# A decoder trunk on Trainium2: U and V expert rows gathered together as 8 KB into five joint buffers, and dense tiles loaded in pairs

## The chip, the cores and the metric

One core of one Trainium2 chip runs the whole kernel. The metric is the device time of one execution, in microseconds. Everything is float32.

## What is computed

Two layers of a hybrid decoder on 512 tokens of width 1024. The mixers (attention, gated DeltaNet, S5) come first in a layer; the change does not touch them. After them comes the PEER layer, cut here to what matters:

```python
def block(xt):                       # 128 tokens
    qry = (xt @ w_query).reshape(128, 8, 2, 128)
    ...                              # 16 of 16384 experts for each of 8 heads: idx, gate
    act = jax.nn.gelu(jnp.einsum('td,thkd->thk', xt, expert_u[idx]))
    return jnp.einsum('thk,thkd->td', gate * act, expert_v[idx])
```

and then a gated embedding, `x = x + sigmoid(rms_norm(x, ple_norm) @ ple_w_gate) * (pe @ ple_w)`. `expert_u` and `expert_v` have 16384 rows of 1024 numbers (4 KB) each per layer.

## The kernel before

**Two ways through PEER.** Half of the 512 tokens (tiles 0 and 1) go the dense way, on TensorE: all 16384 experts are multiplied, in 128 tiles of 128 experts. The unit is the *pair* of such tiles: `pre(p)` multiplies the U tiles of pair p with the tokens (32 matmuls, L1721), ScalarE takes the gelu into one of 12 buffers `act_pair` (L1937), VectorE multiplies it by dense gates (L2133, L2136), and `values(p)` multiplies it with the V tiles (16 matmuls, L1733). SyncE loads the U tiles one by one into four buffers (aT, sT and the halves of bT, L1806) and the V tiles into four slots of `v_tile` (L1827); each load waits until the tile that had its buffer was used. A tile is 512 KB, a row of it 4 KB for each of 128 partitions.

The other half (tiles 2 and 3) goes the sparse way, with rows fetched from the tables. A *row* n is one of 16 choices of one head for 128 tokens: 128 table rows of 4 KB, 512 KB, for U and as much for V. There are 256 rows n in a layer. GpSimd fetches them with indirect DMAs (`fetch`, L2198) into five buffers `u_rows` and five buffers `v_rows`. VectorE makes the *dot* of a U row with the normed tokens (L2093; its line shows as CUSTOM_DVE_ANT_0, or ISA in an order) and later the *addition* of the V row times its weight onto x (L2105).

**Chunks.** Four rows are a *chunk*, 64 in a layer. In chunk c VectorE makes the four dots of c, ScalarE one gelu of four columns (L1909), and VectorE the weights (L2099) and the four additions of chunk c - LAG, with LAG = 2. A U buffer is free after its dot, a V buffer after its addition.

**The order** is one list, made by `tail_order`, which each engine follows in its own code. Steps that matter here:

- First the *hot* steps, 32 of them: VectorE builds one-hot tiles (L2120, L2122), TensorE multiplies them (L1708), ScalarE copies the sums (L1922) and stores them in four stores of 2 MB, `dense_gates` (L1925), in pieces of 1 KB. Chunks 0 to 3 stand behind every eighth hot step, so chunk 3 stands just ahead of the last copy and store. A query of TensorE (L1679) with its copy on ScalarE (L1889) stands ahead of chunk 3.
- GpSimd scatters the gates of the first half (L2208), 112 before its first fetch and four behind each of the chunks 0 to 3.
- SyncE loads the gates (L1811, L1812, 4 x 512 KB) once all stores have landed, and only behind these the U tiles of pair 10.
- Then, in the main part, 1.23 pairs to a chunk, up to chunk 58. ScalarE's order there is the gelu of pair p + 11, which waits for the V products of pair p - 1, and then its part of the chunk.
- Beside them stand the parts of `choose`, the selection of heads for the second half: VectorE work, four parts to a head.
- From chunk 57 on the embedding stands between the chunks: `add`, `scale`, `turn`, `embedded` (TensorE L1773, L1781, ScalarE L1962) and `embedding` (VectorE L2176, L2179).

TensorE may run up to 12 pairs ahead of ScalarE's buffers and waits for `gated`, which VectorE gives three pairs ahead. VectorE and ScalarE are tied by `gelu_done`:

```python
v.wait_ge(s.gelu_done, p + 1)                      # p = c - LAG
act.wait_ge(s.v_done, 2 * (p - AHEAD) + 2)         # in ScalarE's pre(p)
pool.wait_ge(free, n - RINGS + 1)                  # in fetch
```

## Time and profile before

| | us |
|---|---|
| median of 3 runs | 4101.56 (4099.58 to 4101.72) |
| the profiled execution, its own time | 4101.73 |
| its span, first to last instruction | 4099.8 |
| TensorE busy in the span | 3766.2 (92%) |
| VectorE busy | 2532.3 (62%) |
| GpSimd busy | 1789.6 (44%) |
| gathers and scatters (queue q0), share of 16 DMA engines | 35.8% |
| SyncE's loads (queue q1) | 31.3% |

The two layers are alike and take half of the span each. In the page's slices one digit is 102.5 us. In the timeline a row gives start, duration, engine and line; in brackets stands how long the engine sat idle before it and what ended that. In views of waits and of the chain, an arrow points to what was waited for. Some records are missing from a trace, so counts fall a few per cent short.

### The profile page before, as it was taken

The page shows a single profiled execution, that of the slowest core. Times are in us where ns is not written, and L with a number is a line of the kernel's source. Part 1 is how long each engine was busy: PE and PEld are TensorE (multiplying, and loading weights), DVE is VectorE, ACT ScalarE, POOL GpSimd, SP SyncE. Part 2 cuts the span into 40 slices and gives each one's busy share as a digit, 9 for nine tenths or more (in the row PEclk, how much of TensorE's full clock was granted, in tenths as well). Part 3 has the DMA queues.
Part 4 walks back from the last instruction along what each step waited for, and adds up shares of the span by engine and source line. Part 5 has one row for each costly group of instructions (what it writes and reads, how often), then busy time and mean ns, then how long its engine had stood idle before and what let it go on. Part 6 is the DMA issues. An engine that isn't in the chain of part 4 may idle for free. (4 is left out here: it accounts for less than half of the span.)

```text
span 4099.8 us, 43527 instructions
## 1 busy us (share of the span) xinstructions
PE 3766.2 (92%) x15978; PEld 2821.7 (69%) x15978; DVE 2532.3 (62%) x5462; ACT 739.8 (18%) x1381; POOL 1789.6 (44%) x1508
## 2 busy tenths in 40 slices
PE   8999999987899999995799999999878999999947
PEld 7856788876666666652688567888766666666526
DVE  4455215838767676877844452158387677668777
ACT  2243302211000000000222433022111000000002
POOL 3001103777555455555530021037774554555665
PEclk9899999998999999997897999999989999999978
DMA  3301134549999999999623011445599999999996
GB/s 106 113 31 42 58 144 144 134 117 327 409 410 403 409 400 410 406 409 400 235 84 113 31 42 59 145 142 134 124 331 409 410 408 408 402 410 399 409 403 243
DMA packets 332164, 1047.19 MB, mean 255 GB/s; under 512 B 79024, under 2 KB 96048, under 8 KB 313008
## 3 DMA queue, kind: packets, MB, share of 16 engines
q0 software_dynamic: 184320, 537.08, 35.8%
q1 hardware_dynamic: 130576, 488.45, 31.3%
q10 hardware_dynamic: 17056, 18.88, 1.3%
q8 instruction: 128, 2.10, 0.2%
q14 instruction: 84, 0.69, 0.0%
HBM read 1008.49 MB, written 35.78 MB: 255 GB/s over the span
## 5 line engine op out<-in xcount | busy, mean ns | idle before, releaser
L1733 PE MATMUL bank<-v_tile,shared 128*128 128x512 f32 x2048 | 906.2, 597 | 31.9 <-DVE shared L2136 30.2
L2198 POOL DMA_INDIRECT u_rows<-in_peer_u,idx_all x512 | 673.6, 1316 | 541.1 <-DVE act_u L2093 444.5
L2105 DVE SCALAR_TENSOR_TENSOR x<-v_rows,act_w,x 128x1024 f32<-128x1024 f32 x512 | 657.8, 1285 | 349.9 <-DMA v_rows<-in_peer_v,idx_all 331.9
L2093 DVE CUSTOM_DVE_ANT_0 u_rows<-u_rows,h 128x1024 f32<-128x1024 f32 x512 | 610.0, 1221 | 194.8 <-DMA u_rows<-in_peer_u,idx_all 193.1
L1733 PEld LDWEIGHTS bank<-v_tile,shared 128*128 128x128 f32 x2048 | 391.6, 192 | 485.2 <-issue 444.6
L2198 POOL DMA_INDIRECT v_rows<-in_peer_v,idx_all x512 | 560.6, 1095 | 370.7 <-DVE x L2105 275.0
L2208 POOL DMA_INDIRECT first_cells<-first_gate,cell_all x256 | 412.6, 1612 | 593.4 <-DVEq L2085 467.0
L1721 PE MATMUL bank<-hT,bT 128*128 128x256 f32 x2048 | 452.5, 379 | 0.0
L1721 PEld LDWEIGHTS bank<-hT,bT 128*128 128x128 f32 x2048 | 388.4, 190 | 72.0 <-issue 22.0
L1625 PE MATMUL bank<-hT,ring 128*128 128x256 f32 x1536 | 341.6, 383 | 14.3 <-PEq L152 14.2
L1625 PEld LDWEIGHTS bank<-hT,ring 128*128 128x128 f32 x1536 | 293.9, 192 | 56.9 <-issue 16.2
L1367 POOL TENSOR_TENSOR dn_ct<-dn_lt,mixer_consts 128x512 f32<-128x512 f32 x48 | 64.1, 1336 | 593.2 <-ACT dn_lt L1179 458.7
L1721 PE MATMUL bank<-hT,aT 128*128 128x256 f32 x1024 | 236.6, 385 | 33.5 <-DMA aT<-in_peer_ut 33.5
L1937 ACT ACTIVATE shared<-bank 128x512 f32<-128x512 f32 x128 | 76.0, 596 | 975.5 <-PE bank L1733 941.3
L1721 PEld LDWEIGHTS bank<-hT,aT 128*128 128x128 f32 x1024 | 197.5, 194 | 76.7 <-issue 51.4
L1721 PE MATMUL bank<-hT,sT 128*128 128x256 f32 x1024 | 231.5, 379 | 0.0
L1679 PE MATMUL bank<-hT,ring 128*128 128x256 f32 x1024 | 225.9, 379 | 3.5 <-ACT hT L1885 3.5
L1679 PEld LDWEIGHTS bank<-hT,ring 128*128 128x128 f32 x1024 | 194.1, 190 | 34.8 <-issue 7.1
L1721 PEld LDWEIGHTS bank<-hT,sT 128*128 128x128 f32 x1024 | 194.6, 190 | 26.4
L367 PE MATMUL bank<-ring,hT 128*128 128x256 f32 x640 | 151.4, 398 | 0.0
L367 PEld LDWEIGHTS bank<-ring,hT 128*128 128x128 f32 x640 | 150.1, 329 | 1.1 <-issue 0.9
L1653 PE MATMUL bank<-ring,shared 128*128 128x256 f32 x512 | 115.8, 390 | 13.0 <-DVE shared L1993 13.0
(406 smaller groups left out, 4547.8 us busy)
## 6 DMA issues: line engine op xcount, KB each, us to landing
v_tile<-in_peer_v SPq DMA_DIRECT2D x256, 512.0 KB, 7.4
ring<-in_w_in_panels SPq DMA_DIRECT2D x76, 1024.0 KB
bT<-in_peer_ut SPq DMA_DIRECT2D x128, 512.0 KB, 8.1
ring<-in_peer_w_query SPq DMA_DIRECT2D x32, 1024.0 KB
aT<-in_peer_ut SPq DMA_DIRECT2D x64, 512.0 KB, 7.2
sT<-in_peer_ut SPq DMA_DIRECT2D x64, 512.0 KB, 7.0
first_cells<-zeros SPq DMA_DIRECT2D x16, 1024.0 KB, 11.0
ring<-in_w_abv SPq DMA_DIRECT2D x16, 1024.0 KB
```

What stands on the lines that cost most here:

```text
L367: ins = nc.tensor.matmul(bank[:, 0:PANEL], m.hT[:, k, r::4], w[:, k, :], start=(k == 0), stop=(k == KD - 1))
L1367: nc.gpsimd.tensor_tensor(heads(ct[:, i % 2, :]), heads(lt[:, i % NT, :]), over(m.c(f"join{JOINS[i // NT]}").unsqueeze(1), (P, DN, P)), AL ...
L1625: ins = mm(bank[:, cols(mt)], a[:, mt * P:(mt + 1) * P], b[:, cols(half)], start=(n == 0), stop=(n == len(groups) - 1))
L1653: ins = mm(bank[:, cols(t)], comb[:, k, t * P:(t + 1) * P], w[:, k, :], start=(k == 0), stop=(k == KD - 1))
L1679: ins = mm(bank[:, cols(part)], w[:, k, part * P:(part + 1) * P], m.hT[:, k, cols(half)], start=(k == 0), stop=(k == KD - 1))
L1721: ins = mm(pre_bank(p)[:, cols(e % 2)], pre_w[e % DENSE][:, k, :], m.hT[:, k, cols(0)], start=(k == 0), stop=(k == KD - 1))
L1733: ins = mm(acc[t][part][:, :], act_pair[p % AHEAD][:, at:at + P], v_tile[:, e % DENSE, part * 512:part * 512 + 512], start=(e == 0), stop= ...
L1937: f(act_pair[p % AHEAD], pre_bank(p)[:, :], ACT.Gelu_apprx_tanh).then_inc(s.pre_read, 1)
L2093: nc.vector.tensor_tensor_reduce(out=u[:, n % RINGS, :], in0=u[:, n % RINGS, :], in1=h[:, t, :], scale=1.0, scalar=0.0, op0=ALU.mult, op1= ...
L2105: stt(out=m.x[:, 2 + t, :], in0=vr[:, n % RINGS, :], scalar=act_w[:, p % 4, i:i + 1], in1=m.x[:, 2 + t, :], op0=ALU.mult, op1=ALU.add).the ...
L2198: nc.gpsimd.indirect_dma_start(out=rows[:, n % RINGS, :], out_offset=None, in_=table, in_offset=bass.IndirectOffsetOnAxis(ap=idx_all[:, t, ...
L2208: nc.gpsimd.indirect_dma_start(out=cells, out_offset=bass.IndirectOffsetOnAxis(ap=cell_all[:, n:n + 1], axis=0), in_=first_gate[:, 0, n:n ...
```

## The change

1. The host lays U and V rows side by side in one table `peer_uv` (8 KB a row); one indirect DMA fetches both (1 MB) into one of five buffers `uv_rows`. A buffer is free after the addition.
2. LAG and the chunk's two halves are gone: VectorE makes the dot of row n and behind it the addition of row n - 2 (ROWS_BEHIND).
3. ScalarE makes the gelu and the weight row by row, with two small operations in place of one in four, and VectorE's L2099 is gone.
4. The U and V tiles of a pair are one load of 1 MB in rows of 8 KB, two buffers each for U (asT, bT) and V (the halves of v_tile).
5. The fetches in GpSimd's order follow the additions.

```diff
-LAG = 2
+LAG = 1
+ROWS = CHUNKS * STEP
+ROWS_BEHIND = 2
...
-        u = sb("u_rows", [P, RINGS, D])
-        vr = sb("v_rows", [P, RINGS, D])
+        uv = sb("uv_rows", [P, RINGS, 2 * D])
...
+        pre_pair = [a[:, :, :].rearrange("p k n -> p (k n)") for a in (m.asT, m.bT)]
...
             def pre(p):
                 if p == 0:
                     sp.wait_ge(s.comb_ready, KD)
-                for e in range(2 * p, min(2 * p + 2, KEYS)):
-                    if e >= DENSE:
-                        sp.wait_ge(s.pre_done, e - DENSE + 1)
-                    sp.dma_start(pre_w[e % DENSE], io.peer_ut[layer, e]).then_inc(pre_in[e % DENSE], 16)
+                if p == PAIRS_ALL:
+                    return
+                if p >= 2:
+                    sp.wait_ge(s.pre_done, 2 * p - 2)
+                sp.dma_start(pre_pair[p % 2], io.peer_ut[layer, p]).then_inc(pre_in[p % 2], 16)
...
-                for e in (2 * p, 2 * p + 1):
-                    if e >= DENSE:
-                        sp.wait_ge(s.v_done, e - DENSE + 1)
-                    sp.dma_start(v_tile[:, e % DENSE, :], io.peer_v[layer, e * P:(e + 1) * P, :]).then_inc(v_in[e % DENSE], 16)
+                if p >= 2:
+                    sp.wait_ge(s.v_done, 2 * p - 2)
+                at = 2 * (p % 2)
+                sp.dma_start(v_tile[:, at:at + 2, :].rearrange("p a d -> p (a d)"), io.peer_vt[layer, p]).then_inc(v_in[p % 2], 16)
...
             def chunk(c):
-                if c < CHUNKS:
-                    act.wait_ge(s.u_free, STEP * (c + 1))
-                    f(act_g[:, c % 4, :], act_u[:, c % 4, :], ACT.Gelu_apprx_tanh).then_inc(s.gelu_done, 1)
+                if c == CHUNKS:
+                    return
+                for i in range(STEP):
+                    n = c * STEP + i
+                    t, col = slot(n)
+                    one = slice(i, i + 1)
+                    act.wait_ge(s.dotted, n + 1)
+                    f(act_g[:, c % 4, one], act_u[:, c % 4, one], ACT.Gelu_apprx_tanh).then_inc(s.gelu_done, 1)
+                    act.wait_ge(s.gelu_done, n + 1)
+                    f(act_w[:, c % 4, one], act_g[:, c % 4, one], ACT.Copy, scale=gate_all[:, t, col:col + 1]).then_inc(s.weighed, 1)
...
+            def dot(n):
+                t, _ = slot(n)
+                k = n // STEP % 4
+                v.wait_ge(m.uv_landed[n % RINGS], arrivals(n))
+                nc.vector.tensor_tensor_reduce(out=uv[:, n % RINGS, 0:D], in0=uv[:, n % RINGS, 0:D], in1=h[:, t, :], scale=1.0, scalar=0.0,
+                                               op0=ALU.mult, op1=ALU.add, accum_out=act_u[:, k, n % STEP:n % STEP + 1]).then_inc(s.dotted, 1)
+
+            def add_row(n):
+                t, _ = slot(n)
+                k = n // STEP % 4
+                v.wait_ge(s.weighed, n + 1)
+                if n:
+                    v.wait_ge(s.uv_free, n)
+                stt(out=m.x[:, 2 + t, :], in0=uv[:, n % RINGS, D:], scalar=act_w[:, k, n % STEP:n % STEP + 1], in1=m.x[:, 2 + t, :],
+                    op0=ALU.mult, op1=ALU.add).then_inc(s.uv_free, 1)
+                if n % TOPK == TOPK - 1:
+                    v.wait_ge(s.uv_free, n + 1)
+                    v.sem_inc(s.out_free, 1)
+
             def chunk(c):
...
+                for n in range(c * STEP, (c + 1) * STEP):
+                    if n < ROWS:
+                        dot(n)
+                    if ROWS_BEHIND <= n < ROWS + ROWS_BEHIND:
+                        add_row(n - ROWS_BEHIND)
...
                 if n >= RINGS:
-                    pool.wait_ge(free, n - RINGS + 1)
+                    pool.wait_ge(s.uv_free, n - RINGS + 1)
...
+                fetch(n)
+            for c in range(CHUNKS):
+                begin = STEP * (c + 1) - ROWS_BEHIND - STEP + RINGS
+                for n in range(max(begin, RINGS), min(begin + STEP, ROWS)):
+                    fetch(n)
                 if c < LATE_CHUNKS:
                     for n in range(TOPK // LATE_CHUNKS):
                         scatter(late + c * TOPK // LATE_CHUNKS + n)
...
-    a["peer_ut"] = a["peer_u"].reshape(n, KEYS, P, KD, P).transpose(0, 1, 4, 3, 2)
+    a["peer_ut"] = a["peer_u"].reshape(n, PAIRS_ALL, 2, P, KD, P).transpose(0, 1, 5, 2, 4, 3).reshape(n, PAIRS_ALL, P, 2 * D)
+    a["peer_vt"] = a["peer_v"].reshape(n, PAIRS_ALL, 2, P, D).transpose(0, 1, 3, 2, 4).reshape(n, PAIRS_ALL, P, 2 * D)
+    a["peer_uv"] = np.concatenate([a["peer_u"], a["peer_v"]], axis=-1)
```

The parts below are in the order in which instructions stand on an engine, in layer 2 for GpSimd and the end, in layer 1 for the rest. In the new kernel L2101 is the dot, L2110 the addition, L1917 and L1919 ScalarE's two row operations, L2208 the fetch and L2218 the scatter.

GpSimd before, at the first fetches, behind the 112 scatters:

```order
L2198 DMA u_rows<-in_peer_u,idx_all 128x1024 x5
L2198 DMA v_rows<-in_peer_v,idx_all 128x1024 x5
L2198 DMA u_rows<-in_peer_u,idx_all 128x1024 x4
L2208 DMA first_cells<-first_gate,cell_all 4194304x1 x4
L2198 DMA u_rows<-in_peer_u,idx_all 128x1024 x4
```

and now:

```order
L2208 DMA uv_rows<-in_peer_uv,idx_all 128x2048 x7
L2218 DMA first_cells<-first_gate,cell_all 4194304x1 x4
L2208 DMA uv_rows<-in_peer_uv,idx_all 128x2048 x4
L2218 DMA first_cells<-first_gate,cell_all 4194304x1 x4
L2208 DMA uv_rows<-in_peer_uv,idx_all 128x2048 x4
```

Rows 5 and 6 are fetched ahead of the first late scatters and wait for additions 0 and 1; from then on four fetches stand between two groups of scatters.

ScalarE before, from the last hot copies to the last store and the next gelu:

```order
L1922 ACTIVATE gates<-bank 128x128x4 x7
L1889 ACTIVATE query<-bank 128x512
L1909 ACTIVATE act_g<-act_u 128x4
L1922 ACTIVATE gates<-bank 128x128x4
L1925 DMA dense_gates<-gates 2048x1x256
L1937 ACTIVATE shared<-bank 128x512
```

and now (the L1917 and L1919 rows stand four times):

```order
L1932 ACTIVATE gates<-bank 128x128x4 x7
L1892 ACTIVATE query<-bank 128x512
L1917 ACTIVATE act_g<-act_u 128x1
L1919 ACTIVATE act_w<-act_g,gate_all 128x1
...
L1932 ACTIVATE gates<-bank 128x128x4
L1935 DMA dense_gates<-gates 2048x1x256
L1947 ACTIVATE shared<-bank 128x512
```

The last copy and store stand behind four row operations, each of which waits for its own dot.

VectorE before, the last additions of a layer:

```order
L2105 SCALAR_TENSOR_TENSOR x<-v_rows,act_w,x 128x1024 x4
L2176 TENSOR_TENSOR scores<-scores,bank 128x256
L2179 TENSOR_TENSOR x<-x,scores 128x256
L2176 TENSOR_TENSOR scores<-scores,bank 128x256
L2179 TENSOR_TENSOR x<-x,scores 128x256
L2099 TENSOR_TENSOR act_w<-act_g,gate_all 128x4
L2105 SCALAR_TENSOR_TENSOR x<-v_rows,act_w,x 128x1024 x4
L2151 TENSOR_TENSOR shared<-x,gain_ffn 128x1024
```

and now:

```order
L2101 ISA uv_rows,act_u<-uv_rows,h 128x1024
L2101 ISA act_u 128x1
L2110 SCALAR_TENSOR_TENSOR x<-uv_rows,act_w,x 128x1024 x3
L2188 TENSOR_TENSOR scores<-scores,bank 128x256
L2191 TENSOR_TENSOR x<-x,scores 128x256
L2188 TENSOR_TENSOR scores<-scores,bank 128x256
L2191 TENSOR_TENSOR x<-x,scores 128x256
L2163 TENSOR_TENSOR shared<-x,gain_ffn 128x1024
```

Two steps of the embedding (L2176 and L2179, now L2188 and L2191) stood ahead of the last four additions and stand behind all of them now.

## Rows read from the trace of the kernel before

**Rows 1.** The page, busy time, and slices of 102.5 us.

```profile
PE 3766.2 (92%) x15978; PEld 2821.7 (69%) x15978; DVE 2532.3 (62%) x5462; ACT 739.8 (18%) x1381; POOL 1789.6 (44%) x1508
...
PE   8999999987899999995799999999878999999947
...
GB/s 106 113 31 42 58 144 144 134 117 327 409 410 403 409 400 410 406 409 400 235 84 113 31 42 59 145 142 134 124 331 409 410 408 408 402 410 399 409 403 243
```

**Rows 2.** Layer 1: busy PE, PEld, DVE, ACT, POOL; clock, DMA, GB/s.

```profile
1050.00:1800.00 750.00, 750.00 (x2690) 507.52 (x2689) 542.67 (x1028) 59.76 (x140) 395.36 (x337) 1.00 1.02 407
1810.00:1935.00 125.00, 88.77 (x192) 37.87 (x190) 83.29 (x120) 2.25 (x10) 71.11 (x61) 0.87 1.02 408
1975.00:2005.00 30.00, 30.00 (x145) 26.46 (x144) 28.31 (x38) 12.59 (x15) 24.21 (x19) 1.00 0.90 314
```

**Rows 3.** The same view where only weight panels with rows of 8 KB arrive.

```profile
120.00:125.00 5.00, 5.00 (x31) 4.27 (x31) 4.46 (x9) 2.44 (x5) 0.00 (x0) 0.88 1.02 419
```

**Rows 4.** By line, 1050 to 1800: busy, mean ns; idle before, releasers.

```profile
L2105 DVE SCALAR_TENSOR_TENSOR x<-v_rows,act_w,x 128x1024 f32<-128x1024 f32 x168 | 215.9, 1285 | 141.6 <-DMA v_rows<-in_peer_v,idx_all 138.1
L2093 DVE CUSTOM_DVE_ANT_0 u_rows<-u_rows,h 128x1024 f32<-128x1024 f32 x169 | 201.6, 1221 | 57.5 <-DMA u_rows<-in_peer_u,idx_all 57.2
```

**Rows 5.** Waits, 1050 to 1800: us in total, times, longest.

```profile
ACT shared L1937 <- PE bank L1733: 456.5, 36, 13.2
...
ACT act_g L1909 <- DVE act_u L2093: 5.7, 2, 5.2
```

**Rows 6.** Gathers (L2198), 1050 to 1800, from issue to landing.

```profile
DMA to landing us min/median/max: 6.6/17.1/23.6
```

**Rows 7.** Timeline, GpSimd, layer 2: start, us, line; the first gather.

```profile
2963.09 1.00 POOL L2198 DMA_INDIRECT u_rows<-in_peer_u,idx_all  x1 [0.30 <-issue]
```

**Rows 8.** Timeline, DVE, layer 2: chunks 0, 1 and 3.

```profile
2967.28 1.23 DVE L2093 CUSTOM_DVE_ANT_0 u_rows<-u_rows,h 128x1024 f32<-128x1024 f32 x1 [16.15 <-DMA u_rows<-in_peer_u,idx_all]
...
2974.76 0.08 DVE L2093 DVE_READ_ACCUMULATOR2_ANT act_u<- 128x1 f32 x1
...
2991.82 1.21 DVE L2093 CUSTOM_DVE_ANT_0 u_rows<-u_rows,h 128x1024 f32<-128x1024 f32 x1
...
2996.41 0.07 DVE L2093 DVE_READ_ACCUMULATOR2_ANT act_u<- 128x1 f32 x1
...
3032.66 1.21 DVE L2093 CUSTOM_DVE_ANT_0 u_rows<-u_rows,h 128x1024 f32<-128x1024 f32 x1
...
3037.43 5.45 DVE L2105 SCALAR_TENSOR_TENSOR x<-v_rows,act_w,x 128x1024 f32<-128x1024 f32 x4
```

**Rows 9.** Chain that ended last, 3033 to 3086: start, us, what.

```profile
3033.97 6.92 PE bank L1679 x32
...
3042.12 26.41 DMA dense_gates<-gates
...
3070.39 14.85 DMA aT<-in_peer_ut
```

**Rows 10.** Stores of dense_gates, 2970 to 3070, from issue to landing.

```profile
DMA to landing us min/median/max: 8.6/16.0/26.4
```

**Rows 11.** Timeline, DVE, end of layer 2.

```profile
3988.68 1.22 DVE L2093 CUSTOM_DVE_ANT_0 u_rows<-u_rows,h 128x1024 f32<-128x1024 f32 x1 [0.18 <-DVE x L2143]
...
4011.84 1.28 DVE L2163 COPY shared<-bank 128x512 f32<-128x512 f32 x2
...
4066.75 0.41 DVE L2176 TENSOR_TENSOR scores<-scores,bank 128x256 f32<-128x256 f32 x1
...
4068.52 5.45 DVE L2105 SCALAR_TENSOR_TENSOR x<-v_rows,act_w,x 128x1024 f32<-128x1024 f32 x4
```

**Rows 12.** Chain that ended last, 4066 to 4075.

```profile
4067.22 2.08 PE bank L1781 x4
4069.29 5.38 PE bank L1773 x16
```

**Rows 13.** Timeline, TensorE: the first gate product of the embedding.

```profile
4013.33 9.67 PE L1773 MATMUL bank<-ring,shared 128*128 128x256 f32 x32 [9.20 <-issue]
```

More of the change, by code:

```diff
@@ L1605, in arrivals @@
             k = n % RINGS
-            return 16 * (layer * len(range(k, CHUNKS * STEP, RINGS)) + n // RINGS + 1)
+            return 16 * (layer * len(range(k, ROWS, RINGS)) + n // RINGS + 1)
         block = ctx.enter_context(nc.Block())
@@ L2085, in choose @@
                     v.sem_inc(s.selected if half else s.first_chosen, 1)
-            def chunk(c):
-                if c < CHUNKS:
-                    for i in range(STEP):
-                        n = c * STEP + i
-                        t, col = slot(n)
-                        v.wait_ge(m.u_landed[n % RINGS], arrivals(n))
-                        nc.vector.tensor_tensor_reduce(out=u[:, n % RINGS, :], in0=u[:, n % RINGS, :], in1=h[:, t, :], scale=1.0, scalar=0.0,
-                                                       op0=ALU.mult, op1=ALU.add, accum_out=act_u[:, c % 4, i:i + 1]).then_inc(s.u_free, 1)
-                if LAG <= c < CHUNKS + LAG:
-                    p = c - LAG
-                    t, col = slot(p * STEP)
-                    v.wait_ge(s.gelu_done, p + 1)
-                    step.step(tt(act_w[:, p % 4, :], act_g[:, p % 4, :], gate_all[:, t, col:col + STEP], ALU.mult))
-                    for i in range(STEP):
-                        n = p * STEP + i
-                        v.wait_ge(m.v_landed[n % RINGS], arrivals(n))
-                        if n:
-                            v.wait_ge(s.v_free, n)
-                        stt(out=m.x[:, 2 + t, :], in0=vr[:, n % RINGS, :], scalar=act_w[:, p % 4, i:i + 1], in1=m.x[:, 2 + t, :],
-                            op0=ALU.mult, op1=ALU.add).then_inc(s.v_free, 1)
-                    if p % JOB_CHUNKS == JOB_CHUNKS - 1:
-                        v.wait_ge(s.v_free, STEP * (p + 1))
-                        v.sem_inc(s.out_free, 1)
@@ L2188, in _, with fetch @@
         def _(pool):
-            def fetch(n, free, rows, table, sems):
-                if not 0 <= n < CHUNKS * STEP:
-                    return
+            def fetch(n):
                 t, col = slot(n)
@@ L2196, in fetch @@
                 if n >= RINGS:
-                    pool.wait_ge(free, n - RINGS + 1)
+                    pool.wait_ge(s.uv_free, n - RINGS + 1)
                 nc.gpsimd.indirect_dma_start(
-                    out=rows[:, n % RINGS, :], out_offset=None, in_=table,
+                    out=uv[:, n % RINGS, :], out_offset=None, in_=table,
                     in_offset=bass.IndirectOffsetOnAxis(ap=idx_all[:, t, col:col + 1], axis=0),
-                ).then_inc(sems[n % RINGS], 16)
+                ).then_inc(m.uv_landed[n % RINGS], 16)
             def scatter(n):
@@ L2216, in _ @@
             for n in range(RINGS):
-                fetch(n, s.u_free, u, tables[0], m.u_landed)
-            for n in range(RINGS):
-                fetch(n, s.v_free, vr, tables[1], m.v_landed)
-            for c in range(CHUNKS + LAG):
-                for n in range(STEP * c + RINGS, STEP * (c + 1) + RINGS):
-                    fetch(n, s.u_free, u, tables[0], m.u_landed)
-                for n in range(max(STEP * (c - LAG), 0) + RINGS, STEP * (c - LAG + 1) + RINGS):
-                    fetch(n, s.v_free, vr, tables[1], m.v_landed)
+                fetch(n)
[3 more added lines that the diff above has]
+                    fetch(n)
                 if c < LATE_CHUNKS:
@@ L2266, in decoder_trunk @@
                 m.ring = sm("ring", [P, RING, KD * PANEL])
-                m.aT = sm("aT", [P, 2, T])
-                m.sT = sm("sT", [P, 2, T])
+                m.asT = sm("asT", [P, 4, T])
+                m.aT, m.sT = m.asT[:, 0:2, :], m.asT[:, 2:4, :]
                 m.bT = sm("bT", [P, DN, T])
```

19 lines of the change are left out of this document (10 added, 9 removed).

## The prediction

> **What bounds the kernel now.** I read the slices of the page first: in each layer TensorE and the DMA engines are both near full for ten slices, at about 409 GB/s [rows 1]. Then the stretches of layer 1 [rows 2]. From 1050 to 1800 us TensorE has no gap (750 of 750 us) and DMA moves 407 GB/s: two limits that happen to agree. From 1810 to 1935 TensorE has gaps and DMA still moves 408 GB/s: transfers bound this stretch. From 1975 to 2005 DMA is down to 314 GB/s and VectorE is busy 28.3 of 30 us: VectorE bounds it.
>
> Who leads whom in the first stretch: VectorE takes 169 dots and 168 row additions in 750 us, 4.44 us for a row of U and V; of that 1.22 + 0.08 + 1.29 = 2.6 us are work, and most of the rest is waiting for V and U rows [rows 4]. ScalarE waits 456 us for the V products (its buffer for the next activations is free only then) and only 5.7 us for dots [rows 5]. So ScalarE walks in step with TensorE, and VectorE runs ahead of its activations, by up to the two chunks (eight rows) that LAG allows. Ten gathers of 0.5 MB are in flight, which is why one needs 17.1 us to land [rows 6], although an idle machine does it in 4.2 us (issue at 2963.09, dot at 2967.28) [rows 7, 8].
>
> **The faster packets.** A 4 KB row runs at 407 to 409 GB/s; panels whose rows are 8 KB reached 419 [rows 2, 3]. That is 2.4 to 3% where DMA bounds. Over 1050 to 1800 it buys nothing by itself, since TensorE bounds there too.
>
> **The five joint buffers.** A buffer is now held until its V half is added, two rows after its dot. So two to three are with VectorE, and two to three MB are in flight instead of five. For a row to come round: three row periods must hold about 2.6 us of dot and add, 0.3 us to GpSimd, and the landing. The landing alone is 4.2 us for 0.5 MB, of which 1.3 us is data at 409; with 1 MB it is 2.9 + 2.5 = 5.4 us. So 3 periods >= 8.3 us, 2.8 us for a row with nothing beside it. Beside the dense tiles the gather has 419 less 171 GB/s (407 less 169 rows of 1.05 MB in 750 us): 1.05 MB then takes 4.2 us instead of 2.5, and 3 periods >= 10 us plus queueing. The period needed is 4.44 us, 13.3 us for three, so it fits on average, but DMA would have to be full 407/419 = 97% of the time with a queue that runs dry whenever VectorE does a choose part or waits for ScalarE. I take a loss of 6 us a layer, about 1% of this stretch; bounds 0 and 34 (4.6 us a row over 172 rows would be 28, and the present slack is used up first).
>
> **The start of a layer, per layer** (times of layer 2). First, dot 0 needs 1 MB where it needed 0.5, and four rows need 4.2 MB: I take 5 us later for the end of chunk 0, between 3.7 and 6.2 (now 2974.8) [rows 8]. Second, LAG is gone from the front: chunk 1 now has four additions besides four dots. It took 4.6 us (2991.82 to 2996.48) [rows 8]; 8 operations are 10.3, and row 7 is fetched only after addition 2 inside the same chunk, so 11: +6.5. Chunk 2 has the same wait: +0.8. The one-hot work is VectorE's and in series with this, so chunk 3 begins 12.3 us later. Third, in ScalarE's order the query copy stands ahead of chunk 3's activations. It waits for TensorE's 6.92 us query [rows 9], so addition 12 is held, dot 15 comes after it, and the copy and store of the last gates stand behind dot 15: +3.4. The store, now issued at 3042.12, is issued 15.7 us later.
>
> Fourth, the store itself. It takes 26.4 us beside a full gather queue and 8.6 us at best [rows 9, 10]. Its 2 MB are 128 packets of 1 KB on each engine, 206 ns each in that case, about what a 4 KB and a 1 KB packet need together (4 KB at a sixteenth of 409 GB/s is 160 ns, which leaves 46): store and gather take turns by packet. With an 8 KB partner it would be 46 us; with an empty queue, which five buffers often leave, near 8.6. The gather asks for about six rows in that time, which is 15 us of the engines, so I take 20.5: -6. The Trainium skill ("DMA: Bandwidth & Descriptors", Queues, rings and completion order) says that an engine goes round its queues by packet; the 206 ns agree with that. Fifth, the gate tiles and the next U pair, 14.85 us until the load landed [rows 9]: 3 MB in turn with 8 KB gathers, but a thinner queue; I take the same, at most 5 more. TensorE's restart is 12.3 + 3.4 - 6 = 10 us later, between -4 (its pairs 6 to 9, 27.6 us behind the shifted query, end at 3081, now restarted at 3085.2) and +41 (store 46, load 5 more).
>
> **The stretch that DMA bounds** (1810 to 1935). At its start the new kernel has two additions open instead of eight: some 2.5 rows less to fetch. the 130 us up to 1942 at 408 GB/s are 53 MB; 50.3 MB at 419 are 120, with 3% for the short queue 124, and it starts 1 us later: -5, between -11 and +3.
>
> **The VectorE stretch and the end.** From 3988.7 to 4074 VectorE does 24 dots and 32 additions [rows 11]; it will do 26 additions: six times 1.3 us less. Against it stands ScalarE: after the copy at 4011.84 its gate activation waits for TensorE's 9.67 us from 4013.33 on [rows 11, 13], and addition 240 now stands behind it (+4.8), which shortens what the loop of 2.8 us would cost: -4, between -8 and +2. At the very end, two embedding steps (L2176, L2179) stood ahead of the last four additions: done at 4066.75, they let TensorE run 2.1 + 5.4 us beside the additions [rows 11, 12]. Now they stand after the last addition, and TensorE's 7.5 us come in series: +7.
>
> The two small ScalarE operations a row (0.2 us each) and GpSimd's halved number of issues hide: ScalarE is busy 8% and GpSimd 53% of the first stretch [rows 2]. A pair of experts is 32 matmuls like the query's, 6.9 us [rows 9]: the paired load is asked for half of that, 3.5 us, later than the first of two was, and has three such steps, 20 us, until it is used: nothing.
>
> **Sum.** Per layer 10 + 6 - 5 - 4 + 7 = +14 us, twice: +28. The profiled execution took 4101.73 us (span 4099.8), 0.2 from the median 4101.56: 4130 us.
>
> **Rivals.** *The rate wins.* The short queue lets the store through in 9 to 12 us and never runs dry in the transfers' stretch: restart +1, nothing lost in step, then -9, -8, +7: -9 a layer, 4084 us. For it: 419 against 409, and DMA is full half the time. Against: TensorE has no gap for 750 us a layer. 25%. *The queue runs dry* (the other side, further out). It decides from a period above 4.44 us: at 4.6 the stretch in step loses 34 instead of 6 us: 4186 us. For it: DMA must be 97% full with three rows in flight, where ten gave 100%. 20%. The skill's same page (Anatomy of one DMA) gives each transfer a fixed 2.0 us; by it, an estimate, 5 MB in flight or 2.5 differ only if the queue empties, which is this rival. *The gather's rows are cut into 4 KB packets.* All costs, no rate: the gain of 5 us goes and the stretch in step costs 12 instead of 6: 4152 us. 8%. *Costs and gains cancel*, 4094 to 4110: 12%. My forecast: 35%.
>
> **Numbers.** A change under 0.2% (8 us) can't be told from none. Faster: the first rival, 25%. Same: the cancelling case and a little of the forecast's edge, 13%. Slower: 62%. The range goes from 4080 to 4185: it leaves out the best of the first rival and the end of the second.
>
> **What would show it.** Packets of q0: 65,536 of 8 KB in place of 131,072. Chunk 1 near 11 us; store of the last gates issued near 3058 and landed in about 20; TensorE's restart near 3095; still no TensorE gap in the 750 us; VectorE waiting for act_w while ScalarE waits for TensorE; DMA between 400 and 415 GB/s after 1810; TensorE's L1781 and L1773 rows of the last but one unit after the last addition. Landing of a gather near 8 us instead of 17. Wrong it would be if TensorE waits for gates in mid-stretch, or if the restart is not late.

## The result and the profile after

The changed kernel takes 4231.6 us (median of 4 runs, 4229.3 to 4240.5) where the kernel before takes 4101.6 (4 runs): a ratio of 1.0319, 95% interval 1.0301 to 1.0337, 130 us slower. The forecast was 4130 us, its range ended at 4185. The profiled execution is the longest of the four, 4240.5 us with a span of 4238.7.

The page of the changed kernel: busy time, GB/s in slices of 106 us, and the gather's queue (against [rows 1]):

```profile
PE 3813.2 (90%) x15978; PEld 2847.5 (67%) x15978; DVE 2495.2 (59%) x5334; ACT 961.3 (23%) x2277; POOL 1144.3 (27%) x996
...
GB/s 103 110 30 41 74 142 140 139 160 305 378 372 392 401 402 405 378 370 388 213 82 110 30 41 72 143 140 139 169 307 378 372 389 403 412 396 386 386 377 209
...
q0 software_dynamic: 110592, 537.05, 33.8%
```

The 65,536 packets of 8 KB are there (110,592 less 45,056 of the scatters), so the change does what it says. But where the kernel before held 399 to 410 GB/s for nine slices of a layer, the changed one moves 370 to 412.

The stretches of [rows 2], same columns, and the lines of [rows 4], in the changed kernel (L2101 is the dot, L2110 the addition):

```profile
1050.00:1800.00 750.00, 729.20 (x2611) 496.02 (x2610) 500.21 (x931) 128.07 (x416) 181.34 (x160) 0.99 0.96 390
1810.00:1935.00 125.00, 101.40 (x272) 52.88 (x271) 91.45 (x154) 20.82 (x71) 34.22 (x31) 0.92 0.95 384
```

```profile
L2110 DVE SCALAR_TENSOR_TENSOR x<-uv_rows,act_w,x 128x1024 f32<-128x1024 f32 x159 | 203.7, 1281 | 50.3 <-ACT act_w L1919 50.3
L2101 DVE CUSTOM_DVE_ANT_0 uv_rows<-uv_rows,h 128x1024 f32<-128x1024 f32 x159 | 194.4, 1223 | 194.8 <-DMA uv_rows<-in_peer_uv,idx_all 193.5 <-DVE x L2110 0.9 <-DVE gate_all L2094 0.2
```

DMA is no longer full (shares 0.96 and 0.95 for 1.02), 160 rows are fetched in 750 us instead of 169, and the addition waits 50 us for ScalarE, which it did not before [rows 4]. Dots and additions together wait no longer for rows than they did (193.5 us against 57.2 + 138.1), but they now get fewer rows for it. And ScalarE, which waited 456.5 us for the V products and 5.7 us for dots [rows 5], now waits mostly for dots:

```profile
ACT act_g L1917 <- DVE act_u L2101: 390.6, 115, 7.6
...
ACT shared L1947 <- PE bank L1735: 86.7, 18, 14.9
```

So in this stretch ScalarE no longer walks in step with TensorE but behind the rows. The granted clock is 0.99 there for 1.00, so the clock is not the cause.

That DMA falls short in bursts and not evenly shows in the same 750 us cut in 40 slices:

```profile
GB/s 384 226 424 421 419 392 404 219 379 421 408 422 401 420 345 356 421 421 400 423 419 422 333 398 404 379 402 421 410 418 398 353 421 422 333 416 421 339 382 403
```

The best slices move 419 to 424 GB/s, which is the rate that the prediction hoped for; some others move 219 to 356. I read this as a queue that runs dry for some microseconds at a time; no view here shows the queue itself.

**Where the time went.** I compare the start of each chunk's first dot in both traces (after less before) and sum it up for each layer. Of the 9.1 us by which layer 1 starts late, 6.3 stand already at the first U pair of TensorE: the granted clock was 0.73 instead of 0.80 between 100 and 200 us in this execution, ahead of anything that the change touches.

| rows of PEER | layer 1 | layer 2 |
|---|---|---|
| chunk 0 starts late by | 9.1 | 76.1 |
| chunks 0 to 4 | +14.1 | +16.0 |
| chunks 4 to 8 | +18.7 | +19.3 |
| chunks 8 to 11 | -6.2 | -4.9 |
| chunk 11 to 12 | +14.9 | +14.5 |
| chunks 12 to 50 | +20.3 | +16.6 |
| chunks 50 to 58 | -1.3 | -4.2 |
| chunk 58 to the last addition | -0.1 | -0.1 |
| to the next layer's chunk 0, or the end | +6.6 | +5.6 |
| sum | 76.1 | 138.9 |

TensorE's V products tell the same sum in other places: late by 31.7 us from the restart (pair 0) to pair 15 in layer 1, 45.8 at pair 51, 69.5 at the end of pair 63. At pair 51 the rows (chunk 50) are already 70.9 late. TensorE spends its lead over the rows where transfers bound: from 1880 to 1995 its V products wait for VectorE's gate products (L2145 and L2148, 34 us), which stand between the dots and additions in VectorE's order. By the rows that stretch itself loses nothing.

```profile
PE bank L1735 <- DVE shared L2148: 24.5, 4, 10.4
...
PE bank L1735 <- DVE shared L2145: 9.9, 1, 9.9
```

**Chunks 4 to 8.** The last gates' store in layer 2 (ScalarE's queue), its landing, and TensorE's restart:

```profile
3134.84 0.52 ACTq L1935 DMA_DIRECT2D dense_gates<-gates  x1
```

```profile
DMA to landing us min/median/max: 27.0/27.0/27.0
```

```profile
3157.11 9.02 PE L1723 MATMUL bank<-hT,asT 128*128 128x256 f32 x32 [13.04 <-ACT shared L1947]
3165.97 7.07 PE L1723 MATMUL bank<-hT,bT 128*128 128x256 f32 x32
3184.04 9.21 PE L1723 MATMUL bank<-hT,asT 128*128 128x256 f32 x32 [11.01 <-ACT shared L1947]
```

VectorE's dots of chunk 4 there (it has no other work between them but the additions):

```profile
3140.96 1.30 DVE L2101 CUSTOM_DVE_ANT_0 uv_rows<-uv_rows,h 128x1024 f32<-128x1024 f32 x1 [3.66 <-DMA uv_rows<-in_peer_uv,idx_all]
3147.21 1.23 DVE L2101 CUSTOM_DVE_ANT_0 uv_rows<-uv_rows,h 128x1024 f32<-128x1024 f32 x1 [3.74 <-DMA uv_rows<-in_peer_uv,idx_all]
3154.77 1.23 DVE L2101 CUSTOM_DVE_ANT_0 uv_rows<-uv_rows,h 128x1024 f32<-128x1024 f32 x1 [5.13 <-DMA uv_rows<-in_peer_uv,idx_all]
```

Beside the store a row takes 6 to 7.5 us. The DMA queues in the 27.0 us of that store (packets, MB, share of the 16 engines; q0 has gathers and scatters, q10 the store, q1 two U pairs):

```profile
q0 software_dynamic: 1377, 5.91, 60.5%
q10 hardware_dynamic: 2064, 2.10, 23.3%
q1 hardware_dynamic: 288, 2.10, 18.9%
```

The engines are full. In the kernel before they were as full in the 26.4 us of its store, with nearly the same bytes (5.79, 2.10 and 2.10 MB), so the store takes nearly the same time.

ScalarE stands in its order at this chunk's rows, and the gelus of two U pairs stand behind them. TensorE has both banks full and waits for ScalarE, not for its U pair as before.

**Chunk 12.** Both kernels hold ScalarE up here, for a query that TensorE reaches 20 us later. First the kernel before, then the changed one:

```profile
1149.57 1.22 DVE L2093 CUSTOM_DVE_ANT_0 u_rows<-u_rows,h 128x1024 f32<-128x1024 f32 x1
...
1157.97 0.60 ACT L1889 ACTIVATE query<-bank 128x512 f32<-128x512 f32 x1 [20.02 <-PE bank L1679]
```

```profile
1170.18 1.23 DVE L2101 CUSTOM_DVE_ANT_0 uv_rows<-uv_rows,h 128x1024 f32<-128x1024 f32 x1
...
1190.76 1.28 DVE L2110 SCALAR_TENSOR_TENSOR x<-uv_rows,act_w,x 128x1024 f32<-128x1024 f32 x1 [19.34 <-ACT act_w L1919]
```

Before, VectorE goes on with dots of chunk 12 while ScalarE waits; it needs nothing of ScalarE for eight rows. Now it stops two rows after ScalarE does, no buffer comes free, and the gathers stop too.

**The loop of a row.** Gathers in 1050 to 1800 (against [rows 6]):

```profile
L2208 POOL DMA_INDIRECT uv_rows<-in_peer_uv,idx_all x160: 936/937/1954, 1049.2 to 1798.5; - x160
...
DMA to landing us min/median/max: 6.1/9.8/15.0
```

Addition n - 5 frees the buffer of row n. It ends 2.5 us after dot n - 3 began, and the fetch is issued 0.3 us later. So three row periods must hold 2.8 us and the landing: 4.2 us a row at the median of 9.8, 5.9 at the longest of 15.0, where 4.44 are needed. At least half of the gathers come in time, but with little to spare, and the time lost by a late one is hardly made up.

### The profile page after: what moved, and what is told of

It reads as the page before. It is cut to its first block and busy times, and to the rows that moved or that the text cites. A ratio compares the mean times of both kernels' runs of the same rounds, so it can differ in the third digit from the quotient of the medians.

```text
span 4238.7 us, 43511 instructions
## 1 busy us (share of the span) xinstructions
PE 3813.2 (90%) x15978; PEld 2847.5 (67%) x15978; DVE 2495.2 (59%) x5334; ACT 961.3 (23%) x2277; POOL 1144.3 (27%) x996
## 3 DMA queue, kind: packets, MB, share of 16 engines
q0 software_dynamic: 110592, 537.05, 33.8%
## 5 line engine op out<-in xcount | busy, mean ns | idle before, releaser
L2208 POOL DMA_INDIRECT uv_rows<-in_peer_uv,idx_all x512 | 590.8, 1154 | 1668.8 <-DVE x L2110 1644.8
L2101 DVE CUSTOM_DVE_ANT_0 uv_rows<-uv_rows,h 128x1024 f32<-128x1024 f32 x512 | 626.3, 1223 | 613.1 <-DMA uv_rows<-in_peer_uv,idx_all 609.4
L1735 PE MATMUL bank<-v_tile,shared 128*128 128x512 f32 x2048 | 924.9, 606 | 67.5 <-DVE shared L2148 47.4
L2110 DVE SCALAR_TENSOR_TENSOR x<-uv_rows,act_w,x 128x1024 f32<-128x1024 f32 x512 | 655.8, 1281 | 103.8 <-ACT act_w L1919 103.4
L2218 POOL DMA_INDIRECT first_cells<-first_gate,cell_all x256 | 411.0, 1605 | 590.0 <-DVEq L2095 466.0
L1723 PE MATMUL bank<-hT,asT 128*128 128x256 f32 x2048 | 467.3, 388 | 64.7 <-ACT shared L1947 61.8
L1723 PEld LDWEIGHTS bank<-hT,asT 128*128 128x128 f32 x2048 | 397.7, 195 | 139.8 <-ACT shared L1947 69.5
L1723 PEld LDWEIGHTS bank<-hT,bT 128*128 128x128 f32 x2048 | 388.2, 190 | 76.4 <-issue 20.3
L1917 ACT ACTIVATE act_g<-act_u 128x1 f32<-128x1 f32 x512 | 102.6, 200 | 1345.7 <-DVE act_u L2101 1345.1
L1919 ACT ACTIVATE act_w<-act_g,gate_all 128x1 f32<-128x1 f32 x512 | 150.9, 295 | 16.6
L1710 PE MATMUL bank<-shared,gain_ffn 128*128 128x128 f32 x256 | 46.4, 350 | 92.2 <-DVE gain_ffn L2132 81.8
L951 PE MATMUL bank<-hT,ring 128*128 128x512 f32 x256 | 118.4, 618 | 7.9 <-PEq L152 7.9
```

Of the source, the lines that this page charges most:

```text
L951: ins = mm(bank[:, :], w[:, k, mt * P:(mt + 1) * P], m.hT[:, k, :], start=(k == 0), stop=(k == KD - 1))
L1723: ins = mm(pre_bank(p)[:, cols(e % 2)], pre_w[e % DENSE][:, k, :], m.hT[:, k, cols(0)], start=(k == 0), stop=(k == KD - 1))
L1735: ins = mm(acc[t][part][:, :], act_pair[p % AHEAD][:, at:at + P], v_tile[:, e % DENSE, part * 512:part * 512 + 512], start=(e == 0), stop= ...
L1919: f(act_w[:, c % 4, one], act_g[:, c % 4, one], ACT.Copy, scale=gate_all[:, t, col:col + 1]).then_inc(s.weighed, 1)
L2101: nc.vector.tensor_tensor_reduce(out=uv[:, n % RINGS, 0:D], in0=uv[:, n % RINGS, 0:D], in1=h[:, t, :], scale=1.0, scalar=0.0, op0=ALU.mult ...
L2110: stt(out=m.x[:, 2 + t, :], in0=uv[:, n % RINGS, D:], scalar=act_w[:, k, n % STEP:n % STEP + 1], in1=m.x[:, 2 + t, :], op0=ALU.mult, op1=A ...
```

## The experiments

Each was timed in 3 rounds beside the kernel before. Ratios are to it, with 95% intervals.

**Which part of the change.** The dense loads alone (U shown, V alike):

```diff
-                for e in range(2 * p, min(2 * p + 2, KEYS)):
-                    sp.dma_start(pre_w[e % DENSE], io.peer_ut[layer, e]).then_inc(pre_in[e % DENSE], 16)
+                sp.dma_start(pre_pair[p % 2], io.peer_ut[layer, p]).then_inc(pre_in[p % 2], 16)
```

> The kernel before with the second half of the change alone: U and V tiles of a pair as one load of 1 MB in rows of 8 KB; gathers, LAG and additions as before. Theory A (all of the +130 us comes with the joint row buffers): 4075 to 4103 us, TensorE's restart at 3085 +-5 in layer 2, no TensorE gap in 1050 to 1800, and the DMA-bound stretch at 410 to 415 GB/s. Theory B (the pair loads, coarser and with two buffers, cost part of it, since in the changed kernel TensorE waits after its restart): 4120 us or more.

Measured: 4106.4 us, ratio 1.0013 (0.9998 to 1.0029): no difference, though the median lies just above the range of theory A. Its transfers from 1820 to 1940 and 3860 to 3980:

```profile
1820.00:1940.00 120.00, 88.78 (x200) 37.46 (x198) 79.45 (x113) 2.13 (x9) 73.15 (x60) 0.94 1.02 413
3860.00:3980.00 120.00, 86.10 (x188) 35.62 (x186) 79.00 (x112) 1.44 (x7) 68.56 (x58) 0.90 1.02 412
```

The kernel before moves 404 and 409 there. That is 2.2 and 0.7% more over 120 us each, 1 to 3 us, too little to be seen.

The joint gather alone is the same diff the other way round, on the changed kernel.

> The changed kernel with the dense tiles loaded one by one again (512 KB, rows of 4 KB, four buffers each): the joint gather alone. Theory A: 4225 to 4260 us (the changed kernel's 4231 plus up to 25 us for the slower packets of half the bytes). Theory B: 4190 us or less.

Measured: 4209.6 us, ratio 1.0285 (1.0234 to 1.0336). Neither number was met in full: nearly all of the loss is the gather's, but single tiles are rather better than pairs beside it, by 22 us of the medians. The interval reaches the changed kernel's 1.0319, so this difference is likely and not sure.

**Buffers or packets.** Separate buffers again, all else as changed:

```diff
-        uv = sb("uv_rows", [P, RINGS, 2 * D])
+        u = sb("u_rows", [P, RINGS, D])
+        vr = sb("v_rows", [P, RINGS, D])
...
+                    fetch(n, s.dotted, u, tables[0], m.u_landed)
+                        fetch(n - ROWS_BEHIND, s.uv_free, vr, tables[1], m.v_landed)
```

> The changed kernel with separate buffers again: five U buffers, free after the dot, and five V buffers, free after the addition, each with its own gather of 512 KB; additions still two rows behind the dots, row by row on ScalarE, pair loads kept. Theory 'few bytes in flight' (five joint buffers hold two to three rows in flight where ten gave five): 4100 to 4130 us, and the stall of 14 us at chunk 12 (VectorE's addition waits 19 us for ScalarE, which waits for TensorE's query) is refilled from full buffers. Theory 'slack' (VectorE two rows ahead of ScalarE instead of eight): 4170 to 4215 us, with the 19 us waits of the addition for act_w still there and paid.

Measured: 4137.0 us, ratio 1.0091 (1.0063 to 1.0119), between the two theories: some 94 of the 130 us come back. The step at chunk 12 is still there (23 us in layer 1), and about 11 us of it are made up by chunk 55. By the chunks' first dots, separate buffers give back what chunks 12 to 50 lost (-5.2 and -4.9 us in the two layers, where the changed kernel has +20.3 and +16.6) and 11 to 12 us of the 19 in chunks 4 to 8 (now +6.6 and +8.0), but little of chunks 0 to 4 (+11.7 and +11.4).

> The changed kernel with its five joint buffers, but each filled by two gathers of 512 KB in rows of 4 KB, both waiting for the addition. Theory 'few bytes in flight' or 'slack': as the changed kernel, 4225 to 4275 us (the same hold, packets a few per cent slower, the dot may start at half of the row: 1 to 2 us earlier a round). If instead one gather of 1 MB with 8 KB rows is itself what lands late: 4130 to 4200 us.

```diff
+                for part in range(2):
+                        out=uv[:, n % RINGS, part * D:(part + 1) * D], out_offset=None, in_=tables[part],
```

Measured: 4208.9 us, ratio 1.0270 (1.0233 to 1.0307). So the hold counts most. Two gathers and separate buffers have the same packets and requests and differ in the hold alone, and that is 72 us; two requests of 512 KB in place of one of 1 MB are the other 23, with intervals that just touch (1.0307 and 1.0301). This kernel's dot waits only for the first half of its row.

The Trainium skill ("DMA: Bandwidth & Descriptors", Rules for kernel authors) asks for at least 1 MiB a DMA for the most bandwidth. No run here shows a gain by it: from 1050 to 1800 both kernels move 390 GB/s.

**Rows in flight against slack.** ROWS_BEHIND sets both at once: k rows behind leave 5 - k periods for a landing, and k rows of slack over ScalarE.

```diff
-ROWS_BEHIND = 2
+ROWS_BEHIND = 1
```

> The changed kernel with the addition one row behind the dot instead of two (ROWS_BEHIND = 1): a buffer is held a row shorter, so one more of the five is in flight, and VectorE has one row of slack over ScalarE instead of two. Theory 'few bytes in flight': faster than the changed kernel, 4190 to 4220 us, DMA share in 1050 to 1800 above its 0.96. Theory 'slack': slower, 4240 us or more, with more and longer waits of the addition for act_w than its 50 us.

Measured: 4184.6 us, ratio 1.0197 (1.0172 to 1.0221): 47 us faster, and a little faster than either theory said. Both mechanisms show from 1050 to 1800: DMA's share is 0.97 and the waits for rows fall from 193.5 to 119.3 us, while those for act_w rise from 50.3 to 119.9, the longest 23.0 us at chunk 12.

> The changed kernel with the addition three rows behind the dot: a buffer held a row longer, slack of three rows. Theory 'few bytes in flight': 4250 to 4330 us, a row in the first stretch takes over 4.7 us. Theory 'slack': 4200 to 4228 us.

Measured: 4670.1 us, ratio 1.1379 (1.1357 to 1.1401), far beyond what was expected. Its first stretch:

```profile
1050.00:1800.00 750.00, 647.04 (x2223) 439.75 (x2224) 429.63 (x804) 110.02 (x354) 136.46 (x135) 0.93 0.87 331
```

135 fetches in 750 us are 5.56 us a row. Two such periods less the 2.8 us leave 8.3 us for a landing. The loop of a row now bounds everything: TensorE (busy 647 of 750 us) and DMA (0.87) both have gaps, although slack is larger than before.

> The changed kernel with each addition right behind its own dot: five periods, one more than with one row behind (4184 us), but VectorE now waits about 0.8 us in every row for ScalarE's two operations (dot end to weight end was 0.6 us) and follows every stall of ScalarE at once. Row loop alone: 4150 to 4180 us, if VectorE's waits of 0.8 x 512 = 410 us hide in its idle time. If slack now costs more than flight gives: 4190 us or more.

Measured: 4252.3 us, ratio 1.0381 (1.0360 to 1.0403): slower again by 68 us. From 1100 to 1800 VectorE waits 152 times for ScalarE, for rows only 16 times:

```profile
DVE x L2110 <- ACT act_w L1919: 205.3, 152, 25.6
...
DVE uv_rows L2101 <- DMA uv_rows<-in_peer_uv,idx_all: 19.2, 16, 1.9
```

So with five joint buffers the best is one row behind, between a loop too short and no slack.

```diff
-RINGS = 5
-ROWS_BEHIND = 2
+RINGS = 4
+ROWS_BEHIND = 1
```

> The changed kernel with four joint buffers and the addition one row behind: four less one is three row periods for a fetched row to land, as in the changed kernel (five less two). Theory 'row loop' (only the number of periods between the addition that frees a buffer and the dot that needs it counts): 4231 +-25 us, although 1 MB less is held. Theory 'bytes or buffers as such': near the one with the addition three rows behind, over 4350 us.

Measured: 4274.3 us, ratio 1.0423 (1.0400 to 1.0446). That is 90 us slower than with five buffers (four periods) and 396 faster than five buffers with two periods: mainly the number of periods counts, not the number of buffers. But it is 43 us above the changed kernel, outside the +-25 expected. The row of slack that it lacks would fit; no run here separates that from the buffer.

Now slack alone, with separate buffers, where flight stays (LAG and the loops' ends go with it):

```diff
-ROWS_BEHIND = 2
+ROWS_BEHIND = 6
```

> The one with separate U and V buffers (4137 us) with the addition six rows behind the dot instead of two. Flight is the same, VectorE's slack over ScalarE is six rows. If the rest of 37 us above the kernel before is slack: 4095 to 4115 us, and the step of the dots at chunk 12 (28 us in layer 1, taken back over the next 20 chunks) is gone. If it is the row-by-row work itself or the last embedding steps: 4130 to 4145 us.

Measured: 4105.8 us, ratio 1.0012 (0.9996 to 1.0029). The stop is not gone but comes a chunk later (12 and 18 us at chunk 13), and by chunk 20 some 12 us of it are made up in each layer; chunks 0 to 4 cost -0.4 and +1.3 us. The other 31 us are slack, and nothing measurable is left: row-by-row work on ScalarE, pair loads and the order of the embedding together cost at most 12 us, by the interval.

```diff
-LAG = 2
+LAG = 1
```

> The kernel before with LAG = 1: VectorE four to eight rows ahead of its additions becomes up to four; buffers and flight as they are (ten gathers). Theory 'slack' (VectorE's distance to ScalarE): 4115 us or more, with waits for act_g where ScalarE waits 20 us for the query. Theory 'row loop': 4090 to 4105 us, since full buffers take up a stall; in the VectorE-bound end four additions fewer stand open, 2 to 5 us a layer less.

Measured: the kernel before with LAG = 1 takes 4118.6 us, ratio 1.0052 (1.0035 to 1.0069). Slack binds even with ten gathers in flight: from 1050 to 1800 VectorE waits 55.5 us for act_g, which it did not with LAG = 2.

> The kernel before with LAG = 3: twelve rows of slack. LAG = 1 cost 19 us. If slack still binds at two: 4085 to 4096 us. If two chunks cover the longest wait of ScalarE (20 us is under five rows of 4.44 us): 4097 to 4112 us, the four additions more at the end of a layer costing up to 5 us each.

Measured: 4108.3 us, ratio 1.0024 (1.0005 to 1.0044). Two chunks are enough; a third costs a little.

> The kernel before with four U and four V buffers: four periods, 17.8 us at 4.44, with two to four MB in flight. Row loop (landing shrinks with the queue: 9.8 us with three rows of 1 MB in flight): 4100 to 4125 us, as flight is to spare. If the landing of 17 us were the machine's own and not queueing: over 4200 us.

Measured: 4111.3 us, ratio 1.0028 (1.0006 to 1.0050). With U and V apart, four buffers of each cost about 12 us. A gather now lands in 14.6 us at the median: the 17.1 us of [rows 6] are for the most part time in a full queue, not what a gather needs (4.2 us on an idle machine [rows 7, 8]).

**Single causes in the changed kernel.** ScalarE's copy of a query behind the chunk that it stood ahead of:

```diff
+                if what == "query" and n[0] and n[1] >= 2:
+                    held = n
+                    continue
...
+                if what == "chunk" and held:
+                    query(*held)
+                    held = None
```

> The changed kernel, in ScalarE's order the copy of a query of the second half stands behind the chunk that it stood ahead of; nothing else moves. If the wait of ScalarE for TensorE's query (20 us at chunk 12, passed on to the addition as 19.3 us) is a cause: the step of 14 us that the dots take at chunk 12 shrinks to under 6, the wait of act_w in chunk 3 (3.4 us) goes and the last store is issued 3 us earlier; 4200 to 4220 us. If the row loop alone sets the time and catches the stall up anyway: 4225 to 4235 us.

Measured: 4225.0 us, ratio 1.0302 (1.0279 to 1.0325), as little as the other theory said, though the mechanism did what the first said: the step of the dots at chunk 12 fell from 14.9 to 2.6 us (layer 1) and from 14.5 to 1.5 (layer 2). The intervals overlap. In the two profiled executions the span differs by 13.5 us, in the medians by 7. From 1050 to 1800 the waits for act_w fall from 50.3 to 33.6 us and those for rows rise from 193.5 to 200.6: what the stall no longer takes, the rows take in part.

```diff
                 for n in range(max(begin, RINGS), min(begin + STEP, ROWS)):
                     fetch(n)
+                    if c < LATE_CHUNKS:
+                        scatter(late + done)
+                        done += 1
```

> The changed kernel, the 16 late scatters of GpSimd stand one behind each fetch instead of four behind each chunk's fetches. In the changed kernel row 18 is fetched 7.7 us after its buffer is free, because four scatters (1.9 us each) stand ahead. If that sets the front: chunk 5 of a layer starts 5 to 8 us earlier than the changed kernel's and TensorE's restart comes earlier by as much, 4215 to 4225 us. If the store beside the gathers sets it: within 4 us of the changed kernel, 4227 to 4235 us.

Measured: 4233.9 us, ratio 1.0319 (1.0299 to 1.0338). Chunk 5 starts 22.8 and 22.0 us later than in the kernel before, counted from chunk 0, where the changed kernel has 21.7 and 23.8: the place of the scatters costs nothing here.

```diff
-CHUNKS_BESIDE = (0, 2, 4)
+CHUNKS_BESIDE = (3, 4, 5)
```

> The changed kernel, chunks 4 to 6 stand behind pairs 9, 10 and 11 in the order instead of behind 6, 8 and 10, so that ScalarE makes the gelus of pairs 5 to 8 before it waits for the dots of chunk 4. In the changed kernel TensorE's restart at 1067.6 waits for ScalarE, 9 us after its U pair has landed (issue 1049.7, landing 8.7). If ScalarE behind the rows holds TensorE: TensorE's last restart comes 7 to 10 us earlier in each layer. Theory 'TensorE sets the end': 4210 to 4217 us. Theory 'rows set the end' (the dots are 50 us late at chunk 12 where TensorE is 32 late): within 5 us of the changed kernel, 4226 to 4236.

Measured: 4240.1 us, ratio 1.0347 (1.0327 to 1.0368). That is slightly above both ranges. TensorE's last restart in layer 1 is at 1057.57 instead of 1067.58, as expected, but the first V product has a gap of its own and comes only 3.3 us earlier, of which less than 1 us is left at pair 15:

```profile
1057.57 8.59 PE L1723 MATMUL bank<-hT,asT 128*128 128x256 f32 x32 [11.78 <-DMA asT<-in_peer_ut]
...
1089.81 5.63 PE L1735 MATMUL bank<-v_tile,shared 128*128 128x512 f32 x7 [8.94 <-issue]
```

Single tiles with one row behind:

> The changed kernel with one row behind (4184 us) and the dense tiles loaded one by one. With two rows behind, single tiles were worth 22 us. If that was the dense loads' own (a tile of 512 KB asked for and landed earlier): as much here, 4155 to 4170 us. If it was the landing of a joint row beside smaller loads, in a row loop without slack: now that the loop has a period to spare, 4175 to 4190 us.

Measured: 4169.2 us, ratio 1.0180 (1.0145 to 1.0214), 15 us below its partner by the medians, with intervals that overlap (1.0172 to 1.0221). Whether single tiles are better beside joint rows stays open, and so does why.

**Does the end follow TensorE or the rows?** Two candidates made from the kernel before:

```diff
-GATES_AFTER = 9
+GATES_AFTER = 11
```

> A candidate: the kernel before with SyncE's load of the first gates behind the U tiles of pair 11 instead of pair 9 (GATES_AFTER = 11), so that the U tiles of pairs 10 and 11 don't wait for the store of the gates (the 16.9 us gap of TensorE ahead of its restart at 3085.4, which waits for such a tile). ScalarE's gelu at 3080.4, behind chunk 5 and a choose part, then holds TensorE instead: restart 4 us earlier. If TensorE's restart sets the end: 4091 to 4096 us. If the rows do (transfers from 1810 on): 4096 to 4103 us.

Measured: 4106.7 us, ratio 1.0005 (0.9986 to 1.0024): no difference. TensorE's gap is no shorter (18.1 us in layer 2); it waits for ScalarE there instead of a U tile.

```diff
-CHUNKS_BESIDE = (0, 2, 4)
+CHUNKS_BESIDE = (1, 3, 5)
```

> The same candidate with chunks 4 to 6 one pair later in the order (CHUNKS_BESIDE = 1, 3, 5), so that ScalarE makes the gelus of pairs 7 and 8 ahead of chunk 5 and its choose part: TensorE can take U of pair 10 at about 3069, inside the present gap, 7 us of work. If TensorE's restart sets the end: 4085 to 4093 us. If the rows do: 4096 to 4103 us.

Measured: 4102.4 us, ratio 1.0010 (0.9994 to 1.0026). TensorE fills the gap with U of pair 10, and its V products begin 6.0 and 5.9 us earlier than before in the two layers. But the lead is down to 0.4 and 0.9 us at pair 6 already, and stays there. The loss in layer 1:

```profile
1135.15 5.13 PE L1721 MATMUL bank<-hT,aT 128*128 128x256 f32 x16 [3.94 <-ACT shared L1937]
```

```profile
1119.16 0.20 ACT L1909 ACTIVATE act_g<-act_u 128x4 f32<-128x4 f32 x1 [14.80 <-DVE act_u L2093]
```

TensorE waits for ScalarE, which had waited 14.8 us for a dot of chunk 8 and then 11.8 for a choose part; chunks 6 to 10 start 5 to 10 us later in this run. So VectorE, itself later, takes the lead back within six pairs. The run does not carry an earlier TensorE to the end, and whether one that kept its lead would end earlier stays untested. What speaks against it is a wait in the kernel before: from 1800 to 1920 its V products wait 18.4 us for VectorE's gate products (L2136). No version found here beats the kernel before.

## Why the prediction was wrong

The sign, the likelihood of a loss and several terms were right; the size was not: +14 us a layer, where 67.0 and 62.8 were measured. By the prediction's own steps, counted from the start of chunk 0 in each layer, in us, layers 1 and 2:

| term | predicted | measured, by the rows | measured, by TensorE's V products |
|---|---|---|---|
| chunks 0 to 4 | +15.7 | +14.1, +16.0 | |
| store of the last gates, its own time | -6 (20.5) | +0.9, +0.6 (26.7, 27.0) | |
| the front (rows: chunks 0 to 8; V: to pair 0) | +10 | +32.8, +35.3 | +22.6, +24.1 |
| stretch in step (chunks 8 to 50; pairs 0 to 51) | +6 (0 to 34) | +29.0, +26.2 | +14.1, +10.3 |
| transfers' stretch (chunks 50 to 58; pairs 51 to 63) | -5 (-11 to +3) | -1.3, -4.2 | +23.7, +30.6 |
| VectorE's stretch | -4 | -0.1, -0.1 | |
| very end | +7 | +6.6, +5.6 | |

**What was right.** The start: chunk 0, additions inside chunk 1, the query ahead of chunk 3, each within 1.5 us (chunk 0 alone 3.6 and 4.7 for 5; chunk 1 6.8 and 7.3 for 6.5). The last store is issued 14.8 and 16.6 us later, counted from chunk 0, for 15.7. The embedding steps behind the last addition: VectorE waits 8.13 and 6.45 us there for ScalarE, which waits for TensorE. The rate of full slices, 419 to 424 GB/s. Of the signs that were named, the packets, chunk 1, the store's issue and the wait for act_w came; the store's 20 us, a TensorE without a gap in the 750 us (it is busy 729.2) and 400 GB/s or more after 1810 did not.

**What failed, first: the step "it fits on average".** The prediction had the right loop, three periods of 13.3 us, and set it against 10 us "plus queueing" for which it took nothing. The landing was taken as "near 8 us" and is 9.8 at the median, 15.0 at most. The sum is 12.6 against 13.3, a margin of 0.7 us in a loop that is disturbed by 1 to 20 us at every choose part, query and store. The period then needed is no mean but what the late rows need. Measured by the rows, the stretch in step lost 29.0 and 26.2 us for the 6 taken, still inside its bounds. How steep the curve is could not be read from the trace of the kernel before; the runs show it: taking away one period cost 439 us, in spite of a row more of slack, and giving one back gained 47, in spite of a row less. The rival "the queue runs dry" was the right one (20%), but it had this loss in the stretch in step alone, and its price stopped at 4.6 us a row, where 160 rows in 750 us are 4.69.

**Second: the wrong chain for the sum.** I priced the front by TensorE's restart, and the transfers' stretch by bytes alone. But the rows are the longer chain, and their lateness is carried to the end. For chunks 4 to 8 the sum has nothing for the rows, and they lost 18.7 and 19.3 us there; with separate buffers it is 6.6 and 8.0, so the same ring is most of it. At chunk 8 the rows were 33 and 35 us late, where TensorE's V products were 23 and 24. TensorE's lead of 25 and 27 us over the rows ended in the transfers' stretch, where it waits for VectorE. The term of -5 compared two full queues; in that stretch (1883 to 2012 in layer 1) the changed kernel moved 388 GB/s, and the rows won 1.3 and 4.2 us all the same, within the bounds.

**Third: slack.** The prediction says that VectorE runs ahead "by up to the two chunks (eight rows) that LAG allows", and prices LAG only at the front and the end. In the middle it hid a wait of 20 us at chunk 12. The two experiments that change slack alone give its worth: 31 us from two to six rows (separate buffers), 19 us from four to eight (the kernel before).

**The store**, last. Its 20.5 us are about its own 6 (128 packets of 46 ns) and the 15 for the gathers, and the engines did spend 6.3 and some 15 on them. The 2.1 MB of U tiles that SyncE loads beside it (5.1 us of the engines) and the scatters (1 us) were left out; with them the sum comes to about the 27.0 us measured. In the term for VectorE's stretch the six additions saved and the 4.8 us make -3, not -4; measured is -0.1, and why stays open.

The parts of the 130 us are thus some 94 us for joint buffers (separate against changed, 72 of them for the hold alone), some 31 for slack (six rows against two), and a rest of about 5 that is within the uncertainty. They are not independent, since with joint buffers a row of slack is a row of flight.

## What to carry to other kernels

Joining two operands that are needed at different times makes the earlier one's buffer wait for the later use: count the periods between the release and the next use, subtract the work, and compare with the longest landing, not with the mean; a margin of 5% is none. Even that is not enough by itself: one row behind, four periods are 17.8 us, just 2.8 and the 15.0 of the changed kernel's longest landing, and that kernel is still 83 us slower than the one before, with one row of slack. Before a lag between engines is removed, look for the longest wait of the engine behind in the whole trace; it was hidden by that lag. And price a change on each chain that can set the end (here the rows as well as TensorE), since the one that looks full may have a lead to spare. For a store or load beside a full queue, add up the bytes of every queue that runs beside it.

## What the hardware showed

With rows of 8 KB in both queues the best slices from 1050 to 1800 move 419 to 424 GB/s. With 8 KB in the gather's queue and 4 KB in the dense one (the joint gather alone) they move 416 to 419. With 8 KB in the dense queue and 4 KB in the gather's, the transfers' stretch moves 412 to 413 GB/s, and with 4 KB in both 404 to 409.

A store of 2 MB in pieces of 1 KB took 27.0 us beside 8 KB gathers and 26.4 beside 4 KB gathers. In both cases the 16 engines were full and moved the same bytes, some 10 MB, so here the length of the other queues' packets made no difference.

Gathers of 0.5 MB that land in 17.1 us with ten in flight land in 14.6 when only eight are, and the kernel takes 12 us longer (4111 us against 4099).
